# Splitting the last gate step of a hybrid decoder block into two column halves, and moving one gain multiplication across the last scaling

## What is computed

```python
    ple_gate = jax.nn.sigmoid(rmsnorm(x, g_ple[i]) @ w_ple_gate[i])
    x = x + ple_gate * (p[i] @ w_ple_proj[i])
return rmsnorm(x, g_final)          # x * rsqrt(mean(x*x) + eps) * g_final
```

## Time and profile before

| | |
|---|---|
| median of 3 runs | 1798.12 us (1796.77 to 1798.68) |
| the profiled execution, its own time | 1798.73 us |
| its span, first to last instruction | 1797.0 us |
| granted TensorE clock, mean | 0.997 of full speed |
| TensorE busy | 1771.7 us (99%) |
| VectorE / ScalarE / GpSimd busy | 61% / 38% / 51% |

### The profile page before, as it was taken

How to read it: one execution, slowest core, us unless ns; L and a number is a source line. 1 busy time by engine, 2 the same in 40 slices (tenths; PEclk the granted TensorE clock), 3 DMA queues, 4 the chain that set the end, 5 groups by cost and what they waited for, 6 DMA issues and landing times.

```text
span 1797.0 us, 22264 instructions
## 1 busy us (share of the span) xinstructions
PE 1771.7 (99%) x7972; PEld 1452.3 (81%) x7972; DVE 1092.8 (61%) x1945; ACT 681.2 (38%) x1057; POOL 920.4 (51%) x742
## 2 busy tenths in 40 slices
PE   8999999999999999999999999999999999999998
PEld 6777788888888887888888888888888888888886
DVE  7455522457799997852222222235888888888864
ACT  6443322443323222232322222244444444444464
POOL 6423154434337687776666666305666666664200
PEclk9999999999999999999999999999999999999999
DMA  5221132319764544444444444457999999999821
GB/s 200 94 71 60 47 106 96 105 57 386 264 235 145 167 143 135 140 150 150 144 144 146 149 146 136 146 200 279 369 375 363 374 372 368 379 377 382 309 83 47
DMA packets 155565, 360.99 MB, mean 201 GB/s; under 512 B 32064, under 2 KB 73024, under 8 KB 155328
## 3 DMA queue, kind: packets, MB, share of 16 engines
q1 hardware_dynamic: 100976, 257.47, 41.3%
q0 software_dynamic: 34816, 67.41, 10.4%
q10 hardware_dynamic: 19664, 34.70, 5.3%
HBM read 298.44 MB, written 61.01 MB: 200 GB/s over the span
## 4 chain that ended last, share of the span: by engine, by line
PE 95%; DVE 1%; DMA 1%; ACT 1%; another core or an unknown queue 1%; issue 1%; POOL 0%; ACTq 0%; SPq 0%; DVEq 0%
PE pair L791 38%; PE pair L565 18%; PE pair L567 17%; PE pair L566 17%; PE pair L675 1%; PE pair L695 1%; PE pair L757 1%; PE pair L616 1%; DMA raw<-stream 1%; PE pair L665 0%; PE pair L800 0%; PE pair L839 0%; DVE rstd L1306 0%; DVE hl L1330 0%
## 5 line engine op out<-in xcount | busy, mean ns | idle before, releaser
L519 POOL DMA_INDIRECT gates<-gate_val,gate_at x384 | 418.5, 1090 | 202.1 <-issue 103.4
L1448 DVE TENSOR_TENSOR wl<-raw,wh 128x1024 fp32r<-128x1024 f32 x254 | 309.5, 1220 | 346.8 <-ACT wh L940 329.5
L940 ACT ACTIVATE wh<-raw 128x1024 fp32r<-128x1024 f32 x339 | 356.5, 1054 | 132.6 <-PE pair L567 111.5
L791 PE MATMUL pair<-hh,wh 128*128 128x512 f32 x1024 | 399.4, 390 | 1.8 <-ACT gout L1151 1.0
L791 PE MATMUL pair<-hh,wl 128*128 128x512 f32 x1024 | 399.0, 390 | 1.6 <-issue 1.6
L791 PE MATMUL pair<-hl,wh 128*128 128x512 f32 x1024 | 399.1, 390 | 0.0
L502 POOL TENSOR_TENSOR wl<-raw,wh 128x1024 fp32r<-128x1024 f32 x85 | 205.8, 2427 | 319.8 <-ACT wh L940 319.8
L565 PE MATMUL pair<-wh,act_h 128*128 128x512 f32 x768 | 298.9, 389 | 0.0
L567 PE MATMUL pair<-wh,act_l 128*128 128x512 f32 x768 | 298.8, 389 | 0.0
L566 PE MATMUL pair<-wl,act_h 128*128 128x512 f32 x768 | 298.8, 389 | 0.0
L1151 ACT ACTIVATE gout<-pair 128x512 f32<-128x512 f32 x128 | 76.4, 597 | 491.9 <-PE pair L791 450.6
(11 more groups left out here) (247 smaller groups left out, 1936.9 us busy)
## 6 DMA issues: line engine op xcount, KB each, us to landing
raw<-stream SPq DMA_DIRECT2D x338, 512.0 KB
score_dram<-gout ACTq DMA_DIRECT2D x128, 256.0 KB
gates<-zeros SPq DMA_DIRECT2D x48, 512.0 KB, 6.2
score_in<-score_dram SPq DMA_DIRECT2D x128, 192.0 KB
gate<-gates SPq DMA_DIRECT2D x128, 192.0 KB
gates<-gate_val,gate_at POOLq DMA_INDIRECT x384
x<-xT SPq DMA_DIRECT2D x4, 512.0 KB, 6.6
picked<-score_dram,score_at POOLq DMA_INDIRECT x128
```

Source lines behind the costliest of these rows:

```text
L519: nc.gpsimd.indirect_dma_start(gate_list, bass.IndirectOffsetOnAxis(ap=gate_at[:, r, k:k + 1], axis=0), gate_val[:, r, k:k + 1], None).the ...
L791: last = nc.tensor.matmul(psum[u % 2][:], w(weights, U_DENSE + u, c), halves[:, c, :], start=c == 0 and which == 0, stop=c == DC - 1 and w ...
L940: nc.scalar.activation(wh[:, n % SL, :], raw[:, n % RAW, :], ACT.Copy).then_inc(hi_done, 1)
L1448: nc.vector.tensor_tensor(wl[:, n % SL, :], raw[:, n % RAW, :], wh[:, n % SL, :].bitcast(F32), ALU.subtract).then_inc(low_own, 1)
```

## The change

There are now nine steps in a table `STEPS`: the first seven as before, and the last (right half of tile 3) in two of 256 columns each, step 7 (columns 0 to 255 of the half) and step 8 (256 to 511). Every engine's loop runs over this table, so each of the two has its own 24 matmuls (256 columns wide), its own sigmoid, multiplication, addition and square. The square sum of step 7 goes to `ssq3` and is added by VectorE to `bias3` (a new instruction on one column that waits for ScalarE); that of step 8 goes to a new `last_sum`, from which the square root is taken with that bias. `out` takes a list of halves, and the left half of tile index 2 (the one next to last) is now multiplied before `scale3(3)`, the right half after it.

```diff
--- before.py
+++ after.py
@@ -78,6 +78,8 @@
 END_ORDER = (1, 2, 0, 3)
 RAW = 4
 SL = 8
+STEPS = [(half, i, 0, T) for half in range(2) for i in range(TT)]
+STEPS[-1:] = [(1, TT - 1, 0, T // 2), (1, TT - 1, T // 2, T)]
 
 MIX = ["q", "k"]
 for _i in range(PAIRS):
@@ -227,7 +229,8 @@
         ssq3 = sb("ssq3", [P, 2, TT], F32)
         bias3 = sb("bias3", [P, TT], F32)
         std3 = sb("std3", [P, TT], F32)
-        spare = sb("spare", [P, 2 * TT + 1], F32)
+        last_sum = sb("last_sum", [P, 1], F32)
+        spare = sb("spare", [P, 2 * TT + 2], F32)
 
         gate_at = sb("gate_at", [P, TT - 1, HK], U32)
         gate_val = sb("gate_val", [P, TT - 1, HK], F32)
@@ -892,21 +895,23 @@
                     pe.wait_ge(x_copied, 3)
                     turn2(3)
 
-            def ple_gate(half, i):
-
-                tile, step = END_ORDER[i], TT * half + i
+            def ple_gate(step):
+
+                half, i, first, end = STEPS[step]
+                tile = END_ORDER[i]
                 cols = slice(tile * P, (tile + 1) * P)
                 if half == 0:
                     pe.wait_ge(hl2_ready, 2 * (i + 1))
                 if step >= 2:
                     pe.wait_ge(sg_ready, step - 1)
-                bank = psum[6 + step % 2].rearrange("p (j w) -> p j w", j=4)
+                bank = psum[6 + step % 2][:, 0:end - first].rearrange("p (j w) -> p j w", w=P)
+                js = slice(first // P, end // P)
                 for c in range(DC):
                     n = U_GATE + 4 * half + c // 2
                     if i == 0 and c % 2 == 0:
                         wait_low(pe, n)
                     last = three(bank, hh[:, c, cols], hl[:, c, cols],
-                                 weights(wh, n, 2, c % 2, "p (j k w) -> p k j w"), weights(wl, n, 2, c % 2, "p (j k w) -> p k j w"),
+                                 weights(wh, n, 2, c % 2, "p (j k w) -> p k j w")[:, js], weights(wl, n, 2, c % 2, "p (j k w) -> p k j w")[:, js],
                                  c == 0, c == DC - 1)
                 last.then_inc(gate_ready, 1)
 
@@ -917,12 +922,11 @@
                     pe.wait_ge(out_ready, 2 * (i - 1))
                 turn(xt[END_ORDER[i]], i % 2, turned3, 1 if i == TT - 1 else None)
 
-            for half in range(2):
-                for i in range(TT):
-                    ple_gate(half, i)
-                    if half == 1 and i == 2:
-                        turn3(0)
-                        turn3(1)
+            for step in range(len(STEPS)):
+                ple_gate(step)
+                if step == TT + 2:
+                    turn3(0)
+                    turn3(1)
             turn3(2)
             turn3(3)
 
@@ -1257,26 +1261,29 @@
                 nc.scalar.activation(std3[:, i:i + 1], ssq3[:, 1, i:i + 1], ACT.Sqrt, bias=bias3[:, i:i + 1],
                                      scale=1.0 / D).then_inc(std3_ready, 1)
 
-            for step in range(2 * TT):
-                half, i = divmod(step, TT)
+            for step, (half, i, first, end) in enumerate(STEPS):
                 nc.scalar.activation(spare[:, step:step + 1], eps[:], ACT.Sigmoid)
                 act.wait_ge(gate_ready, step + 1)
                 if step >= 2:
                     act.wait_ge(upd_ready, step - 1)
-                nc.scalar.activation(sg[:, step % 2, :], psum[6 + step % 2], ACT.Sigmoid).then_inc(sg_ready, 1)
-                if step == 2 * TT - 1:
-                    nc.scalar.activation(spare[:, 2 * TT:], eps[:], ACT.Sqrt)
+                nc.scalar.activation(sg[:, step % 2, 0:end - first], psum[6 + step % 2][:, 0:end - first], ACT.Sigmoid).then_inc(sg_ready, 1)
+                if step == len(STEPS) - 1:
+                    nc.scalar.activation(spare[:, step + 1:step + 2], eps[:], ACT.Sqrt)
                 act.wait_ge(x3_ready, step + 1)
                 if step >= 1:
                     act.wait_ge(squared3, step)
-                nc.scalar.activation(squares[:, 0:T], xt[END_ORDER[i]][:, half * T:(half + 1) * T], ACT.Square,
-                                     accum_out=ssq3[:, half, i:i + 1]).then_inc(squared3, 1)
+                total = ssq3[:, half, i:i + 1] if step < len(STEPS) - 1 else last_sum[:]
+                nc.scalar.activation(squares[:, 0:end - first], xt[END_ORDER[i]][:, half * T + first:half * T + end], ACT.Square,
+                                     accum_out=total).then_inc(squared3, 1)
                 if step == TT + 1:
                     act.wait_ge(bias_ready, 1)
                     std3_of(0)
                     std3_of(1)
-                elif step > TT + 1:
+                elif step == TT + 2:
                     std3_of(i)
+            act.wait_ge(squared3, len(STEPS))
+            act.wait_ge(bias_ready, 2)
+            nc.scalar.activation(std3[:, TT - 1:TT], last_sum[:], ACT.Sqrt, bias=bias3[:, TT - 1:TT], scale=1.0 / D).then_inc(std3_ready, 1)
             act.wait_ge(rstd3_ready, TT)
             right = xt[END_ORDER[TT - 1]][:, T:D]
             nc.scalar.activation(right, right, ACT.Copy, scale=std3[:, TT - 1:TT]).then_inc(right3, 1)
@@ -1668,9 +1675,9 @@
                 part = xt[END_ORDER[i]][:, 0:T] if i == TT - 1 else xt[END_ORDER[i]]
                 nc.vector.tensor_scalar(part, part, std3[:, i:i + 1], None, ALU.mult).then_inc(left3, 1)
 
-            def out(i):
-
-                for half in range(2):
+            def out(i, halves=(0, 1)):
+
+                for half in halves:
                     k = 2 * i + half
                     dve.wait_ge(turned3, k + 1)
                     if k >= 4:
@@ -1678,17 +1685,17 @@
                     bank, g = gained(psum[2 * (i % 2) + half], 3, half)
                     nc.vector.tensor_tensor(outb[:, k % 4, :].rearrange("p (c t) -> p c t", c=4), bank, g, ALU.mult).then_inc(out_ready, 1)
 
-            for step in range(2 * TT):
-                half, i = divmod(step, TT)
+            for step, (half, i, first, end) in enumerate(STEPS):
                 tile = END_ORDER[i]
                 dve.wait_ge(sg_ready, step + 1)
                 dve.wait_ge(emb_out, 2 * TT)
                 if step >= 2:
                     dve.wait_ge(x3_ready, step - 1)
-                nc.vector.tensor_tensor(upd[:, step % 2, :], sg[:, step % 2, :], emb[half][:, tile, :], ALU.mult).then_inc(upd_ready, 1)
+                change = upd[:, step % 2, 0:end - first]
+                nc.vector.tensor_tensor(change, sg[:, step % 2, 0:end - first], emb[half][:, tile, first:end], ALU.mult).then_inc(upd_ready, 1)
                 dve.wait_ge(upd_ready, step + 1)
-                part = xt[tile][:, half * T:(half + 1) * T]
-                nc.vector.tensor_tensor(part, part, upd[:, step % 2, :], ALU.add).then_inc(x3_ready, 1)
+                part = xt[tile][:, half * T + first:half * T + end]
+                nc.vector.tensor_tensor(part, part, change, ALU.add).then_inc(x3_ready, 1)
                 if step == TT - 1:
                     dve.wait_ge(squared3, TT)
                     nc.vector.tensor_scalar(bias3[:], ssq3[:, 0, :], 1.0 / D, EPS, ALU.mult, ALU.add).then_inc(bias_ready, 1)
@@ -1699,8 +1706,13 @@
                     out(0)
                     scale3(2)
                     out(1)
+                elif step == TT + 3:
+                    dve.wait_ge(squared3, step + 1)
+                    nc.vector.scalar_tensor_tensor(out=bias3[:, i:i + 1], in0=ssq3[:, 1, i:i + 1], scalar=1.0 / D,
+                                                   in1=bias3[:, i:i + 1], op0=ALU.mult, op1=ALU.add).then_inc(bias_ready, 1)
+            out(2, (0,))
             scale3(3)
-            out(2)
+            out(2, (1,))
             out(3)
```

## The result

The changed kernel took **1811.60 us** in the median (1808.45 to 1813.02, 6 runs) against 1797.35 us (1795.10 to 1798.68, 6 runs) for the kernel before: a ratio of 1.0079, 95% interval 1.0068 to 1.0090. That is 14 us slower, where the forecast was 1797.8 us and "same", and outside the range.

A forecast was written before the change was run, and what follows sets the result against it. TensorE was taken as the bound, busy 1771.7 of 1797.0 us, with only the end able to move. Scaling 0.59 us later, offset by the early store (-0.21, or -0.31 by bytes), gave -0.3 from 1798.12: 1797.8 us, range 1796.5 to 1800.1.

The forecast's parts named there:

- The step that failed: Whole kernel: TensorE's work stays the same up to the last gate step at 1781.25 us; only the last 16 us move.
- The chain of the end: From the last gate matmul to the end: last scaling 0.59 us later, last store issued at 1793.28 against 1793.29.
- Gate step in two: Last gate step on TensorE: 48 matmuls of 256 columns, one every 0.12 us, paced like L800's; ends 0.4 us later.
- rivals 2 and 3: Last gate step: weight loads bound each pair at 0.19 us, 1800.1 us, or aren't hidden, 0.225, 1802.0; chance 0.04 each.
- What holds the last sigmoid: ScalarE, end: step 7's square waits for VectorE's addition behind `out(1)`; last sigmoid at 1788.02 instead of 1787.01.
- Rival 4: Last gate step: split works in full, last sigmoid waits only for TensorE at 1787.4; 0.6 us saved, 1797.2; chance 0.04.
- The scaling: VectorE's last scaling at the end: 1790.97 against 1790.38, 0.59 us later.
- Moving the multiplication: VectorE, end: one gain multiplication ahead of the last scaling costs nothing; three stores stay behind, last landing 3.0 instead of 3.2.
- rival 1: Stores at the end: the early store is worth nothing; +0.6 us at most, 1798.7; chance 0.18.
- The sum: End of the kernel: -0.21 us by issue and landing, -0.31 by bytes; taken as -0.3 us.
- The range: Whole kernel time: from 1796.5 us (forecast and the fastest run's scatter) to 1800.1 us (weight loads at 0.19 us).

The follow-up runs named there:

- pad32: Kernel before plus only an unused 32-byte tensor behind `spare`, moving every later buffer by 32 bytes: 1812.60 us against 1798.39, ratio 1.0083.
- packed: Changed kernel with `last_sum` as the eleventh column of `spare`, so no buffer moves against the kernel before: 1799.08 us against 1798.39, ratio 1.0008.
- sigfirst: packed, with ScalarE's sigmoid of the second half step ahead of the first half's square: 1793.60 us against 1794.07, ratio 0.9993.
- aligned: Kernel before with buffers placed so every pair of large matmul operands is a multiple of 256 bytes apart: 1793.02 us against 1794.07, ratio 0.9995.
- pad512: Kernel before with 512 unused bytes behind `spare`: 1794.30 us against 1793.95, ratio 0.9996.

## Why the prediction was wrong

**The step that failed** is the first: "The change leaves its work alone up to the last gate step, at 1781.25 us, so only the last 16 us can move." It is true of the instructions and false of what they take. The new one-column tensor moved `act_h` and `act_l` by 32 bytes against `wh`, and 2304 matmuls 55 to 580 us ahead of the change took 0.0066 us more each, 15 us (pad32 alone reproduces it, packed alone removes it). No rival had this in it: all of them were about the last 16 us. The diff's two lines on `last_sum` and `spare` never entered the sum, though every line of a diff should. The kernel before even had the sign of it, and the prediction made nothing of it: the same form of matmul at 389 ns in most stages and at 395 to 396 with `conv_h` and `attn_h`.

**The chain of the end was right.** Times since the sigmoid of step 6, in us:

| | before | forecast | after |
|---|---|---|---|
| gate matmul of 256 columns, one every | | 0.12 | 0.1196 |
| last gate matmul ends | 6.88 | 7.3 | 7.15 |
| last sigmoid starts | 6.91 | 7.92 | 7.91 |
| last scaling starts | 10.28 | 10.87 | 10.75 |
| end of the span | 16.90 | 16.6 | 16.48 |

- *Gate step in two:* L800 was the right neighbour. The weight load hides behind 256 columns; rivals 2 and 3 (0.19 and 0.225 us) are out. The Trainium skill's rule (TensorE: Matmul & The Clock Gate, What overlaps and what doesn't) that a weight load overlaps a matmul in flight only when the row group differs doesn't hold for these loads, at 256 columns as at 512. The Trainium skill's 262 cycles for 256 columns (same page, Back-to-back issue gap), an estimate of 0.109 us at 2.4 GHz, are short of the measured 0.1196. The 7.3 us for the last gate matmul were 0.15 too late, 0.10 of it because the forecast left the second matmul at its old start (1.46 us after the sigmoid), though the first one, now half as wide, lets it start at 1.36. It decided nothing, as TensorE isn't last there.
- *What holds the last sigmoid:* the square of step 7 waiting for VectorE's `out(1)`, as the prediction had it: `upd` at 1799.42, one gain multiplication after the other until then, and sigfirst removes it. Rival 4 is out.
- *The scaling* was 0.47 later instead of 0.59. The 1.47 us from table load to square were taken from a square that in the kernel before was waiting for VectorE's addition (which ends at 1789.07 in the earlier trace rows); undisturbed it is 1.41 (1.40 in sigfirst). The rest are some hundredths in the shorter sigmoid and square.
- *Moving the multiplication:* 0.85 us by itself, as the three stores instead of four had it; rival 1, that an early store is worth nothing, is out. A term was missed: with one multiplication in front of them instead of two, the last pair waits for the transposes (`outb` at 1804.90 is 0.83 behind the one before, instead of 0.60), which costs 0.23. So the last store was issued at 13.30 after the sigmoid of step 6, where the forecast had 13.18. In return it landed 2.7 us after its issue instead of the 3.0 I took.
- *The sum:* -0.42 us (after) and -0.08 (packed) around the forecast of -0.3. That it came so near is in part luck, since the missed wait and the faster landing have opposite signs. The halves alone are +0.46 (forecast 0.6), the move alone -0.85 (forecast 0.9). The change joined a loss to a gain of twice its size.
- *The range:* its upper end has a slip in it. Rival 2 is 2.6 us past the forecast of 1797.8, so 1800.4 and not 1800.1. The measured 1811.60 lies far outside either.

## What to carry to other kernels

A diff also changes the memory map: before forecasting "nothing moves elsewhere", compare the start addresses of all buffers in the two programs, and where matmuls of one form have two durations, look at the distance of their operands. In this kernel, keeping the two operands of every large float32r matmul a multiple of 256 bytes apart is worth 3% of the matmul, and costs a few hundred bytes in a partition. And before splitting a last step, ask what an in-order engine will do between the two halves: here the square of the first half held up the second sigmoid, and the split lost 0.46 us. With that square out of the way (sigfirst) the last scaling still came 0.37 us later than with the whole step.

## What was not expected of the hardware

- **The distance of the operands.** A matmul of 128x512 (float32r, the type in which these operands are declared) starts every 0.2257 us when stationary and moving operand are a multiple of 256 bytes apart in their partition, and every 0.2315 to 0.2325 at 32, 64 and 128 bytes beyond one (value stage; `xh`, above, is slowed only in part at 64). The weight loads' records stay at 188 ns in both. The Trainium skill (SBUF — State Buffer, Operand start alignment) asks an operand's address only for a multiple of its element size, and says that this is about legality and not speed; all runs here keep that rule, and their speeds differ. Why the distance counts (how the two reads share the memory) no run here shows. Other types weren't tried, nor narrower matmuls at another distance than 0, nor all distances.
- **The clock before the last transposes.** Between the transposes of the two last tiles TensorE idles some 3.2 us. In after it kept its full clock through them; stretches as before:

```profile
1803.00:1804.00 1.00, 0.00 (x0) 0.00 (x0) 0.50 (x2) 0.74 (x4) 0.00 (x0) 1.00 0.32 95
1804.00:1805.30 1.30, 1.09 (x8) 0.86 (x8) 1.15 (x3) 0.39 (x1) 0.00 (x0) 1.00 0.44 129
```

In packed, with the same instructions and an idle time of the same length, the granted clock fell to the half (1.2 GHz) just before them, and the eight transposes took 1.97 us instead of 1.09:

```profile
1791.00:1792.00 1.00, 0.00 (x0) 0.00 (x0) 0.47 (x1) 0.96 (x5) 0.00 (x0) 1.00 0.00 0
1792.00:1793.00 1.00, 0.04 (x1) 0.04 (x1) 0.74 (x3) 0.77 (x2) 0.00 (x0) 0.77 0.55 167
1793.00:1794.00 1.00, 1.00 (x5) 1.00 (x6) 0.51 (x1) 0.14 (x1) 0.00 (x0) 0.50 0.32 95
...
1792.96 1.97 PE L842 MATMUL pair<-ident,x 128*128 128x128 f32 x8 [3.25 <-DVE x L1676]
```

The last two multiplications came 0.45 and 0.71 us later than in after, the last store was issued at 14.01 instead of 13.30, and it landed in 2.4 us instead of 2.7, so that 0.34 is left: packed's end was 16.82 us and not 16.48. One profile can't settle a term of 0.3 us here. Of the 17 profiles ten have these last eight transposes in 1.09 us, four in 1.49 to 1.73, and three (packed, aligned, pad512) in 1.97. In aligned and pad512, which have two multiplications ahead of the last pair instead of one, the last store is issued 0.36 us later than in the kernel before and lands 0.3 sooner, and the end is 16.89 and 16.94 us. Which an execution gets, these runs don't tell.
